# Differential attention in one block with its projections: mask and distance in DVE's row-minimum operation, mix factors and evictions once per head

## The reference

```
# H = 8 heads, dh = 64, two maps per head, lambda_init = 0.2
q, k, v = split(rmsnorm(x, norm_mix_2) @ w_in)             # 1024 -> 3 x 1024
q = rmsnorm(q.reshape(B,T,H,2,dh), q_gain) * dh**-0.5
k = rmsnorm(k.reshape(B,T,H,2,dh), k_gain)
lam = exp(sum(lq1*lk1)) - exp(sum(lq2*lk2)) + lambda_init
for s in range(0, T, 128):                                 # 4 query blocks, keys 0..s+128
    sc = q[s:s+128] . k[:s+128]                            # per head and map
    dist = query_pos - key_pos
    sc = where(dist >= 0, sc - slope[h]*dist, -inf)        # slope[h] = 2**-(h+1)
    p = softmax(sc)
    out = (p[map 0] - lam * p[map 1]) @ v
o = rmsnorm(out, subln) * (1 - lambda_init)                # per head, over 128
x = x + o.reshape(B,T,1024) @ w_out
```

## Time and profile before

| | |
|---|---|
| median of three runs | 1700.43 us |
| profiled execution | 1699.22 us, span 1697.4 us |
| mean granted clock of TensorE | 0.959 |
| PE busy | 1594.5 us (94%) |
| DVE busy | 800.2 us (47%) |
| ScalarE busy | 680.8 us (40%) |
| GpSimd busy | 59.5 us (4%), all of it in DMA issue and four memsets |
| DMA | 224.71 MB, mean 132 GB/s |

### The profile page before, as it was taken

The page is one execution under the profiler, slowest core; times in us unless marked ns, Lnnn a source line. Parts: engine busy times, 40 slices in busy tenths (PEclk is TensorE's granted clock), DMA queues, the critical chain, the costliest instruction groups (busy, mean ns, idle before and its releaser), DMA issues. The chain is left out here.

```text
span 1697.4 us, 19308 instructions
## 1 busy us (share of the span) xinstructions
PE 1594.5 (94%) x7381; PEld 1279.2 (75%) x7381; DVE 800.2 (47%) x940; ACT 680.8 (40%) x915; POOL 59.5 (4%) x36
## 2 busy tenths in 40 slices
PE   8999999998899889999999979999998849999996
PEld 7988888887666678888888868886656638888885
DVE  6433333224463324333332134345465358888884
ACT  5322222113343324222221133334464228777774
POOL 0000000000000000000000000000000012112111
PEclk9999999999999999999999999997699969999999
DMA  5222222222210112222223212230001298999994
GB/s 213 75 99 99 99 99 92 103 88 89 75 50 1 63 50 97 88 91 95 99 99 100 99 50 100 99 100 16 1 1 50 82 369 322 382 390 390 377 392 112
DMA packets 35731, 224.71 MB, mean 132 GB/s; under 512 B 5175, under 2 KB 5431, under 8 KB 11344
## 3 DMA queue, kind: packets, MB, share of 16 engines
q1 hardware_dynamic: 30912, 210.54, 33.1%
q0 software_dynamic: 4608, 13.22, 3.3%
q10 hardware_dynamic: 144, 0.03, 0.0%
HBM read 213.70 MB, written 13.63 MB: 134 GB/s over the span
## 5 line engine op out<-in xcount | busy, mean ns | idle before, releaser
L233 DVE TENSOR_TENSOR WL<-raw,WH 128x2048 fp32r<-128x2048 f32 x93 | 212.8, 2291 | 456.4 <-ACT WH L228 456.4
L238 PE MATMUL PS<-AH,WL 128*128 128x512 f32 (+2 forms) x776 | 289.7, 373 | 6.2 <-DVE AL L382 4.3
L239 PE MATMUL PS<-AL,WH 128*128 128x512 f32 (+2 forms) x776 | 289.0, 372 | 0.0
L240 PE MATMUL PS<-AH,WH 128*128 128x512 f32 (+2 forms) x776 | 289.0, 372 | 0.0
L228 ACT ACTIVATE WH<-raw 128x2048 fp32r<-128x2048 f32 x93 | 177.2, 1908 | 248.1 <-PE PS L240 245.6
L1962 DVE TENSOR_TENSOR WEL<-eraw,WEH 128x2048 fp32r<-128x2048 f32 x96 | 216.7, 2286 | 17.6 <-ACT WEH L1900 17.6
L1900 ACT ACTIVATE WEH<-eraw 128x2048 fp32r<-128x2048 f32 x96 | 181.6, 1912 | 19.8 <-PE PS L240 18.8
L238 PEld LDWEIGHTS PS<-AH,WL 128*128 128x128 f32 (+1 forms) x776 | 146.5, 189 | 33.0 <-DVE AL L382 4.5
L240 PEld LDWEIGHTS PS<-AH,WH 128*128 128x128 f32 (+1 forms) x776 | 146.5, 189 | 25.8
L239 PEld LDWEIGHTS PS<-AL,WH 128*128 128x128 f32 (+1 forms) x776 | 146.6, 189 | 25.3
L238 PE MATMUL PS<-WH,AL 128*128 128x512 f32 (+1 forms) x384 | 147.8, 385 | 9.9 <-DVE WL L233 4.4
(11 more groups left out here) (310 smaller groups left out, 2267.2 us busy)
## 6 DMA issues: line engine op xcount, KB each, us to landing
eraw<-experts SPq DMA_DIRECT2D x96, 1024.0 KB, 12.7
raw<-stream SPq DMA_DIRECT2D x94, 1024.0 KB, 4.8
moe_rows<-moe_rows_g SPq DMA_DIRECT2D x5, 512.0 KB, 13.8
X<-x SPq DMA_DIRECT2D x4, 512.0 KB, 5.8
out<-X SPq DMA_DIRECT2D x1, 2048.0 KB, 20.1
ffn_row<-rows SPq DMA_DIRECT2D x2, 512.0 KB, 9.3
final_row<-rows SPq DMA_DIRECT2D x2, 512.0 KB, 5.2
pool_bands<-band SPq DMA_DIRECT2D x1, 544.0 KB
```

The source lines that it names most:

```text
L233: dve.tensor_tensor(WL[:, u % SLOTS, :], raw[:, u % SLOTS, :], WH[:, u % SLOTS, :].bitcast(F32), ALU.subtract).then_inc(unit_lo, 1)
L238: pe.matmul(acc, lhs_lo, rhs_hi, start=start, stop=False)
L239: pe.matmul(acc, lhs_hi, rhs_lo, start=False, stop=False)
L240: return pe.matmul(acc, lhs_hi, rhs_hi, start=False, stop=stop)
```

## The change

- Q is scaled by -2^(h+1) times the gain (new constant `unslope`), the distance table becomes positive, and one DVE operation per map does `(PSUM + distance) * slope`, writes it to SBUF, and gives the row minimum. ScalarE takes exp(-x + minimum) in place. Slope products, slope matrices and row maxima are gone.
- Probabilities stay in SBUF for all steps of a head (`buffer`), two heads deep; the mix trails by five steps and is done in place; factors are made once per head; the mix is not divided by the total of map 0 at eviction: one eviction of 128 x 512 per head, and the norm takes the division in.
- Head squares move from ScalarE to GpSimd (multiply, two halving additions) and a DVE reduction.
- The transpositions of q and k stand between the products of band 5; lambdas are made in `da_in`; everything is one `nc.Block`, and SP queues all loads up to the end at once. Weight units are split at steps 3 and 7.
- The output projection works by token tiles up to the split, and takes the product order of the first attention's output.

```diff
-    put("alibi", np.where(dist >= 0, -dist, NEG))
+    put("alibi", np.where(dist >= 0, dist, -NEG))
+    put("unslope", -(2.0 ** (8.0 * np.arange(1, H + 1) / H))[None, :])
...
+        def differential_attention():
+            with ExitStack() as held, nc.Block() as block:
...
+                def buffer(i, m):
+                    h, q = divmod(i, T)
+                    if q < T - 1:
+                        at = 768 * (h % 2) + P * q * (q + 1) // 2
+                        return half[:, m, at:at + (q + 1) * P]
+                    if h % 2:
+                        return square[:, m, :]
+                    return half[:, m, 1536:2048]
+
+                da_in(block, held, QK, V, QT, KT, square, ls, unsloped, lam_ready, v_here, qk_here)
+                da_attend(block, QT, KT, V, O, buffer, total, stat, ls, held, lam_ready, v_here, qk_here, scores_read,
+                          heads_out, squared)
+                da_out(block, O, total, stat, heads_out, squared)
...
 # da_in, PE, behind each tile's products
+                            if b == 5:
+                                pe.wait_ge(normal, T)
+                                for n in range(8 * part + 2 * t, 8 * part + 2 * t + 2):
+                                    if n >= 4:
+                                        pe.wait_ge(qk_emptied[n % 2], (n - 4) // 2 + 1)
+                                    for tile in range(T):
+                                        mm = pe.transpose(PS[:, 4 + n % 4, tile * P:(tile + 1) * P],
+                                                          QK[:, tile, n * P:(n + 1) * P], ident)
+                                    mm.then_inc(turned, 1)
...
 # da_attend, PE
+                def scores(i):
+                    h, q = divmod(i, T)
+                    if q == 0:
+                        pe.wait_ge(qk_here[h % 2], 5 + h // 2)
+                    if i < 2:
+                        pe.wait_ge(v_here, 22 + 2 * i)
+                    else:
+                        pe.wait_ge(maxed, 2 * (i - 1))
+                    for m in range(2):
+                        rows64 = slice(m * 64, m * 64 + 64)
+                        pe.matmul(PS[:, 2 * (i % 2) + m, 0:(q + 1) * P], QT[rows64, h, q * P:(q + 1) * P],
+                                  KT[rows64, h, 0:(q + 1) * P], start=True, stop=True).then_inc(scored, 1)
...
+                scores(0)
+                for i in range(N + 6):
+                    if i + 1 < N:
+                        scores(i + 1)
+                    if 0 <= i - 5 < N:
+                        turn(i - 5)
+                    if 0 <= i - 6 < N:
+                        weigh(i - 6)
...
 # da_attend, DVE
+                for i in range(N + 5):
+                    h, q = divmod(i, T)
+                    if i < N:
+                        w = (q + 1) * P
+                        if i >= 2 * T:
+                            dve.wait_ge(turned, i - 2 * T + 1)
+                        for m in range(2):
+                            dve.wait_ge(scored, 2 * i + m + 1)
+                            dve.tensor_tensor_reduce(buffer(i, m), PS[:, 2 * (i % 2) + m, 0:w],
+                                                     const("alibi")[:, S - w:S], 2.0 ** (-8.0 * (h + 1) / H), -NEG * 1e8,
+                                                     ALU.add, ALU.min, least[:, 2 * i + m:2 * i + m + 1]
+                                                     ).then_inc(maxed, 1)
+                    if q == 1 and 1 <= h <= H:
+                        mine = slice(T * (h - 1), T * h)
+                        dve.wait_ge(exped, 2 * T * h)
+                        dve.reciprocal(factor[:, 1, mine], total[:, 1, mine]).then_inc(factored, 1)
...
+                    j = i - 5
+                    if 0 <= j < N:
+                        dve.scalar_tensor_tensor(buffer(j, 0), buffer(j, 1), factor[:, 0, j:j + 1], buffer(j, 0),
+                                                 ALU.mult, ALU.add).then_inc(combined, 1)
+                    if i in (3, 7):
+                        split_lo(dve, U_DA_OUT + i // 4)
+                    if q == 2 and h >= 3:
+                        sum_squares(h - 3)
+                    if q == 2 and h >= 2:
+                        head_out(h - 2)
...
 # da_attend, GpSimd
+                for h in range(H):
+                    pool.wait_ge(heads_out, h + 1)
+                    if h:
+                        pool.wait_ge(squared, h)
+                    pool.tensor_tensor(head_junk[:, :, :], head_cols(h), head_cols(h), ALU.mult).then_inc(head_square, 1)
...
 # da_out, PE
+                for t in range(T):
+                    turn_heads(t)
+                pe.wait_ge(unit_lo, u0 + 2)
+                for d in range(2):
+                    for t in range(T):
+                        if d == 0:
+                            pe.wait_ge(b.lo, t + 1)
+                        mm = unit_into(d, t)
+                    mm.then_inc(unit_used, 1)
+                pe.wait_ge(unit_lo, u0 + 4)
+                for t in range(T):
+                    mm = unit_into(2, t)
+                    if t == T - 1:
+                        mm.then_inc(unit_used, 1)
+                    mm = unit_into(3, t)
+                    mm.then_inc(made if t < T - 1 else unit_used, 1)
...
 # da_out, DVE, behind six small dependent operations
+                normal_tile(0)
+                normal_tile(1)
+                lo_tile(0)
+                normal_tile(2)
+                lo_tile(1)
+                normal_tile(3)
+                lo_tile(2)
+                lo_tile(3)
```

More of the change, by code:

```diff
@@ L1152, in _ @@
                                 split_lo(dve, u)
[L1155 to L1227, removed]
@@ new lines, in da_in @@
+            turned = sem("da_turned")
+            lam_here = sem("lam_here")
+            lam_step = sem("lam_step")
+            lam_exp = sem("lam_exp")
+            exp_loaded = sem("da_exp_loaded")
+            stat = sb("da_stat", [P, T, 32], where=held)
+            root = sb("da_root", [P, T, 32], where=held)
+            lam = sb("lam", [P, 4, 64], where=held)
+            gained = final_norm(block)
+            _, _, turned_lo = normalize(block, "n4", QK[:, :, 0:D], "mix2", (U_DA, U_DA + 1), QK[:, 0:2, D:2 * D],
+                                     lambda engine, t: engine.wait_ge(gained, t + 1), act_tiles=range(T))
@@ new lines, in home, with _ @@
+            def home(n):
+                return (QT[:, n, :], unsloped[:, n:n + 1]) if n < 8 else (KT[:, n - 8, :], gain_col("da_k"))
+            @block.sync
+            def _(sp):
+                sp.dma_start(lam[:, :, :].rearrange("p a n -> p (a n)"),
+                             lams.broadcast_to([P, 256])).then_inc(lam_here, 16)
+                for u in range(U_DA + 2, U_DA + 6):
+                    load_unit(sp, u)
+                sp.wait_ge(gained, T)
+                sp.dma_start(final_row[:, :], rows[2:3, :].broadcast_to([P, D])).then_inc(moe_gain_here, 16)
+                for u in range(U_DA + 6, U_END):
+                    load_unit(sp, u)
@@ new lines, in _ @@
+            @block.tensor
+            def _(pe):
+                for b in range(6):
+                    for part in range(2):
+                        u = U_DA + 2 * b + part
+                        pe.wait_ge(unit_lo, u + 1)
+                        for t in range(T):
+                            bank = (4 * (b % 2) if b < 4 else 0) + t
+                            if b >= 2 and part == 0:
+                                pe.wait_ge(emptied, 4 * (b - 2 if b < 5 else 4) + t + 1)
+                            for k in range(4):
+                                c = 4 * part + k
+                                if b == 0 and t == 0:
+                                    pe.wait_ge(turned_lo, c + 1)
+                                w = slice(k * 512, (k + 1) * 512)
+                                mm = product(pe, PS[:, bank, :], AH[:, c, t * P:(t + 1) * P],
+                                             AL[:, c, t * P:(t + 1) * P], WH[:, u % SLOTS, w], WL[:, u % SLOTS, w],
+                                             c == 0, c == C - 1)
+                            if part and t < T - 1:
+                                mm.then_inc(made, 1)
+                            if t == T - 1:
[9 more added lines that the diff above has]
+                                    mm.then_inc(turned, 1)
@@ L2142, in build_program @@
+        differential_attention()
         recycle()
```

418 lines of the change are left out of this document (257 added, 161 removed).

## The result

| | before | after |
|---|---|---|
| median | 1700.34 us | 1671.76 us (1670.9 to 1677.7, four runs) |
| ratio | | 0.9839, 95% interval 0.9816 to 0.9861 |
| profiled execution | 1699.22, span 1697.4 | 1677.7, span 1675.9 |
| first score, on the span | 1166.9 | 1165.0 |
| first score to end of the last weighing | 120.8 | 88.8 |

The forecast was 1678 us. The profiled execution is the slowest of the four, 6 us over their median, so its parts add up to 7 us less gain than the medians have (28.6 us): -1.9 - 32.0 + 12.4 = -21.5 us. Where the executions of one kernel lie more than 1.5% above its fastest, the ratios in this document leave them out.

What follows compares the result with a forecast made beforehand. PE was taken to bound both halves of the attention, with the clock deciding much of the time. Start -3.8, attention -33.8, end +12.3 give -25.3; 3 added for a half-clock spell: -22, 1678 us (own range 1669 to 1689; all 1663 to 1705).

Steps and rivals of the forecast that it cites:

- The attention's 87 us: Second attention: eight heads of 9.4 us plus 12 us of waits at full clock, against 120.8 before.
- rival B: Attention scores: the two maps overlap on PE, saving 1.4 us a head, 11 us in all: 1667 us; chance 0.25.
- the signs the prediction named: Attention: head period 9.4 us (8 if maps overlap), clock near 1.00, fused operation near 0.7 us; also start and output-projection signs.
- Slope products, PE's head of 9.4 us: Attention on PE: removing 64 slope products saves 2.8 us a head at full clock, leaving 9.4.
- DVE: Attention: fused mask, distance and minimum operations take 4.2 us a head; DVE's head of 7.8 stays under PE's 9.4.
- The two splits, 3 us: Attention, blocks 3 and 7: PE waits for DVE's weight split, 2.4 us, with two score buffers ahead; 3 us given.
- A short spell at the half level, 3 us: Allowance added to the full-clock sum of -25.3 us for a short spell at half clock, giving -22.
- The sum of the stage: Attention: 8 x 9.4 + 12 = 87 us, the 12 being 3 splits, 5 last blocks, 4 small waits.
- Start, -3.8: Before the first score: transpositions move between projection products, gaps go, first score at 1163.1 in place of 1166.9.
- End: Last weighing through output projection: +4.6 for a later first product, +1.3 half clock, +6.4 for unit order; +12.3 us.
- Rival A: Attention: clock falls to half; three or four heads low give 1700 us (chance 0.15), nearly all 1738 (0.09).

Runs made afterwards that it cites:

- experiment 2: The changed kernel plus an 8-column, 128-row product between the two maps' score products of each block: median 1722.3 us, ratio 1.0033 to the kernel before.
- experiment 5: The changed kernel with both weight splits moved out of the attention, before the first score and behind the last head: 1660.99 us, ratio 0.9778.
- Experiment 7: The changed kernel with two output projection orders, separately: third and fourth unit one after the other, 1664.91 us; first-unit products between the tiles' transpositions, 1667.98 us.

## Why the prediction was right, and for which part by other means

The time, 1678 against 1671.8, lies inside the forecast's own range, and the sums for the start and for the end were right. The attention's 87 us (88.8 in the profiled execution, 82.5 in a quieter one of the same code) came out of terms that were wrong in opposite directions; that they nearly cancel is luck. 1671.8 is also as near to rival B's 1667 as to the forecast, and of the signs the prediction named, the head period of 8.5 us is B's and the clock near 1.00 did not come (0.85).

- *Slope products, PE's head of 9.4 us.* The removed work was nearly right: 9.8 without overlap (experiment 2), since the slope products' own price was 2.2 us a head and not 2.8. But rival B is what happened, in full. It was given 0.25 and 1.4 us a head, because only the second record of map 0 was taken to lie over the first of map 1. Measured, the whole map 1 lies beside map 0, 2.85 us of PE a head. The row that pointed to it was there (idle weight loads); experiment 2 shows it. The Trainium skill ("TensorEngine Tiling (Array Packing)", Key Properties) says that different tiles can load and multiply in parallel; four records in 1.13 us agree, and so does the return to 2.31 us for a pair (1218.35 to 1220.66) with one 128-row product between.
- *DVE.* 3.9 us a head (4.2 predicted), not the bound by its busy time (60.8 of 88.8 us). It became the last wait of each head all the same: with PE at 6.95 us, the mix of 384 columns is late by 1.35 to 1.55 us. In DVE's stream it stands behind the head's eviction and the two fused operations of 512 columns, which follow one another without a gap.
- *The two splits, 3 us.* This is the step that failed in size: 9.6 us of idle PE, 12.1 us of time (experiment 5). The prediction took DVE's 2.4 us from the earlier trace rows, less two buffered blocks. It left out that DVE first waits in its own stream for ScalarE's half, 2.88 us. Both clock falls of the first half (6.8 us each) lie around these stalls, in every profiled execution that has the splits there with the slope products gone and the maps side by side.
- *A short spell at the half level, 3 us.* 27.3 us of the attention were low, in short pieces: 13.7 around the splits, 13.7 later. The later heads that had them take 10.1 where the others take 8.5: for such a head +1.6, and 6.3 us in all against the quieter execution of the same code (88.8 and 82.5). What keeps the clock up isn't shown. What the profiled executions show is this: where the maps do not overlap, 20.5, 47.8, 58.0, 61.4, 102.4 and 119.5 us of the attention are low; where they do, 0 to 27.3.
- *The sum of the stage.* Eight heads at 9.4 and 12 us of extras were predicted. Measured are the seven periods 3.5, 11.4, 15.1, 8.0, 10.1, 8.5, 10.1 = 66.7 us, and 22.1 from the last head's first score to the end. That is less for each head and more for splits, clock and mix.
- *Start, -3.8.* Right: -3.7 from the stage's own beginning. On the span only 1.9 are seen, because the execution was 1.8 us late where the stage begins.
- *End.* GpSimd 2.5 (2.4 measured), normalising 5.4 after the last weighing (5.4), first product 16.4 (16.3), idle at the third unit 4.4 (4.38), half level 1.3 + 2.0 (12.4 - 4.5 - 4.4 = 3.5 left for it). The sum, 12.3, is 12.4. Experiment 7 shows that both orders had a price: 6.9 us, and some 4 for the other (by its profile).
- *Not foreseen:* GpSimd's additions slow DVE's mix. It costs 0.2 us a head.
- *Rival A* did not decide here, but it was close: with experiment 2's edit most executions fall to it (median 1722 us).

## What to carry to other kernels

When two products use different rows of the array, look at what stands between them: one 128-row product there, even of 8 columns, costs the overlap, and removing it can bring more than its own time. A producer that waits for another engine inside a stream costs the wait and the work, not the work alone: price a moved weight split by both halves in series. When versions differ by clock, compare one head at one level of the granted clock, and the medians only afterwards.

## What the runs showed of the hardware

- Two f32 products on rows 0 to 63 and 64 to 127, two records each, stream side by side: four records of 512 columns in 1.13 us, of 128 in 0.49.
- A PE with work for 117.72 of 118 us of f32 score products, transpositions and weighings stayed at a granted clock of 0.50, while the same work with the maps side by side and PE idle 12.4 of 67.7 us stayed at 1.00. Being busy does not bring the clock back by itself. Nor does it take the clock down: in the kernel before, heads in which PE was busy for 63.67 of 64 us (1216 to 1280) ran at 1.00.
- DVE's mix with both inputs in SBUF, 384 columns: 613 ns alone, 1.14 us when a GpSimd addition of 256 columns (0.72 us) starts with it.
- DVE's fused add, scale and row minimum out of PSUM costs no more than a plain row reduction of the same width (688 and 692 ns at 512 columns).
